# Five operand buffers in the down products of a transformer pair, and their neighbours in the order

## What is computed

```python
def conv_ffn(h, w_up, conv_w, conv_b, w_down):
    u = h @ w_up
    up = jnp.pad(u, ((0, 0), (CONV_WIDTH - 1, 0), (0, 0)))
    u = sum(up[:, i:i + T] * conv_w[i] for i in range(CONV_WIDTH)) + conv_b
    gate, val = jnp.split(u, 2, axis=-1)
    return (jax.nn.gelu(gate, approximate=True) * val) @ w_down

f = conv_ffn(rms_norm(h, norm_ffn_pre[l]), ffn_w_up[l], ffn_conv_w[l], ffn_conv_b[l], ffn_w_down[l])
h = h + rms_norm(f, norm_ffn_post[l])
...
def second_block(x, w_in, pool_w, pool_scale, attn_sinks, w_out, norm_pre, norm_post):
    h = rmsnorm(x, norm_pre[layer])
    proj = h @ w_in[layer]
    pool_u, pool_gate, q, k, v, attn_gate = jnp.split(proj, splits, axis=-1)
    pool_out = pool_mixer(pool_u, pool_w[layer], pool_scale[layer]) * jax.nn.silu(pool_gate)
    ...
```

## Time and profile before

| | us |
|---|---|
| median of three runs (lowest, highest) | 2544.6 (2544.19, 2546.92) |
| the profiled execution, its own time | 2542.34 |
| span of the profiled execution | 2540.5 |
| PE busy in the span | 2394.3 |
| DVE, POOL, ACT busy | 1269.2, 750.4, 694.0 |

### The profile page before, as it was taken

One profiled execution on the slowest core, in us unless ns is written; L12 is line 12 of the kernel. 1 busy time (PEld: TensorE's weight loads), 2 busy tenths in 40 slices (PEclk: granted clock), 3 DMA queues, 4 the chain that ended last, 5 costly groups with the idle time before them and its releaser, 6 DMA issues.

```text
span 2540.5 us, 33655 instructions
## 1 busy us (share of the span) xinstructions
PE 2394.3 (94%) x12944; PEld 1927.0 (76%) x12944; DVE 1269.2 (50%) x1446; ACT 694.0 (27%) x1076; POOL 750.4 (30%) x397
## 2 busy tenths in 40 slices
PE   5999999999999999999999999999999988989895
PEld 3788878877887887877787788888777766767674
DVE  6643263426434534766567544554421567636723
ACT  3422232222223113333243211111123444024421
POOL 1311231122113212113465333333244434322132
PEclk9999999999999999999999999999999999999997
DMA  3211111111111116545443111111143332111011
GB/s 122 70 42 59 68 50 56 53 59 59 51 59 59 50 50 194 185 145 191 141 158 116 42 50 50 41 50 50 41 150 98 108 95 76 53 50 42 26 42 66
DMA packets 58654, 201.00 MB, mean 79 GB/s; under 512 B 5936, under 2 KB 10160, under 8 KB 57776
## 3 DMA queue, kind: packets, MB, share of 16 engines
q1 hardware_dynamic: 39408, 134.56, 17.0%
q10 hardware_dynamic: 19136, 64.80, 6.8%
HBM read 163.16 MB, written 36.18 MB: 78 GB/s over the span
## 4 chain that ended last, share of the span: by engine, by line
PE 77%; DVE 12%; ACT 4%; DVEq 3%; issue 2%; DMA 1%; POOL 0%; ACTq 0%; POOLq 0%; SPq 0%
PE psg L442 10%; PE psg L441 10%; PE psg L437 10%; PE psg L570 5%; PE psg L568 5%; PE psg L563 5%; PE psa L660 1%; PE psg L1099 1%; PE psg L1104 1%; PE psb L649 1%; PE psg L1106 1%; PE psa L500 1%; PE psb L656 1%; DVE rw_SC L1337 1%; PE psg L466 1%
## 5 line engine op out<-in xcount | busy, mean ns | idle before, releaser
L378 POOL CAST whi<-wraw 128x1024 fp32r<-128x1024 f32 (+1 forms) x168 | 180.3, 1073 | 1537.9 <-PE psg L563 558.6
L380 POOL TENSOR_TENSOR wlo<-wraw,whi 128x1024 fp32r<-128x1024 f32 (+1 forms) x168 | 444.7, 2647 | 26.3 <-issue 6.3
L442 PE MATMUL psg<-xhi,wlo 128*128 128x512 f32 x1120 | 447.4, 400 | 0.0
L437 PE MATMUL psg<-xhi,whi 128*128 128x512 f32 x1120 | 441.7, 394 | 4.9 <-DVE pu L1754 2.6
L441 PE MATMUL psg<-xlo,whi 128*128 128x512 f32 x1120 | 442.8, 395 | 0.0
L570 PE MATMUL psg<-xhi,wlo 128*128 128x512 f32 x640 | 260.7, 407 | 0.0
L568 PE MATMUL psg<-xlo,whi 128*128 128x512 f32 x640 | 260.6, 407 | 0.0
L563 PE MATMUL psg<-xhi,whi 128*128 128x512 f32 x640 | 258.6, 404 | 0.0
L437 PEld LDWEIGHTS psg<-xhi,whi 128*128 128x128 f32 x1120 | 210.7, 188 | 57.6 <-issue 6.7
L441 PEld LDWEIGHTS psg<-xlo,whi 128*128 128x128 f32 x1120 | 210.8, 188 | 54.7 <-issue 0.7
L442 PEld LDWEIGHTS psg<-xhi,wlo 128*128 128x128 f32 x1120 | 210.8, 188 | 48.5
(11 more groups left out here) (549 smaller groups left out, 4527.8 us busy)
## 6 DMA issues: line engine op xcount, KB each, us to landing
wraw<-w SPq DMA_DIRECT2D x216, 512.0 KB, 3.6
later_scratch<-stage ACTq DMA_DIRECT2D x40, 512.0 KB, 2.6
xres<-xt ACTq DMA_DIRECT2D x4, 1024.0 KB, 10.8
RV<-later_scratch SPq DMA_DIRECT2D x4, 1024.0 KB, 11.9
RG<-later_scratch SPq DMA_DIRECT2D x4, 1024.0 KB, 6.3
later_scratch<-rstage ACTq DMA_DIRECT2D x8, 512.0 KB, 2.6
mgr<-later_scratch ACTq DMA_DIRECT2D x8, 512.0 KB, 3.9
mgt<-later_scratch ACTq DMA_DIRECT2D x8, 512.0 KB, 4.8
```

Of the source, the lines that this page charges most:

```text
L378: pool.tensor_copy(whi[:, u, 0:width], wraw[:, u, 0:width])
L380: pool.tensor_tensor(wlo[:, u, 0:width], wraw[:, u, 0:width], whi[:, u, 0:width].bitcast(F32), ALU.subtract).then_inc(w_ready, 1)
L437: mm = pe.matmul(ps[:, cols], whi[:, slot, w_cols], rhs_hi(k, cols), start=(k == 0), stop=False)
L442: mm = pe.matmul(ps[:, cols], wlo[:, slot, w_cols], rhs_hi(k, cols), start=False, stop=(k == kts - 1))
```

## The change

1. **Five buffers.** The operand parts of the second pass and of the tail go through a ring of `RING` = 5: two in the old place (now interleaved as `fparts`), three in `fhi_more` and `flo_more`, which lie in the first halves of `ff` tiles 16 to 21, read for the last time in the first pass. ACT and DVE make the parts three steps ahead of PE, and in a step ACT now copies the weights first.
2. **Residual tiles a step later on ACT.** The squares go two a step in steps 2 to 5, the sums on PE come after step 6 and the spread after step 8. DVE's `early_residual` starts in step 9, ACT's `early_high` in step 10, each one tile a step. The sums of the new squares (`mix_square`) stand in steps 18 to 21 instead of in the tail. In the tail a square follows each third part, as before.
3. **First step on the other banks.** The first `down` block takes output tiles 4 to 7 first, whose banks are not those that DVE still reads, and waits for the two others before tiles 0 and 2 only. DVE and ACT take the last hidden tile apart: gate taps ahead of the value, Gelu before the second weights copy, value behind it.
4. **Residual load in eight parts** of 512 KB, one after each pair of blocks.
5. **Second block.** `sums_of` of the second half comes after seven of the first `mix_block`'s eight slices, not after four. `pu` for pooled group 2 is taken from PSUM before DVE waits for group 1's map, and group 1 keeps its pooled values in `pu2`.

```diff
@@ -243,7 +245,9 @@
-        fhi, flo = tiles("fhi", 26, [P, 2, HALF], F32R), tiles("flo", 27, [P, 2, HALF], F32R)
+        fparts = tiles("fparts", 26, [P, 2, 2, HALF], F32R)
+        fhi, flo = fparts[:, :, 0, :], fparts[:, :, 1, :]
+        fhi_more, flo_more = tiles("fhi_more", 16, [P, 3, 2, HALF], F32R), tiles("flo_more", 19, [P, 3, 2, HALF], F32R)
...
+        def part_slot(two, more, n):
+
+            r = (n - FT) % RING
+            return two[:, r, :] if r < 2 else more[:, r - 2, 0, :]
...
@@ -952,10 +961,13 @@
-                for j in range(KT):
+                js = (4, 5, 6, 7, 0, 1, 2, 3) if start else range(KT)
+                for j in js:
                     w_cols = slice(j * P, j * P + P)
+                    if start and j in (0, 2):
+                        pe.wait_ge(g_free[j // 2], T_P2 // 2 + 1)
...
-            pe.wait_ge(g_free[0], T_P2 // 2 + 1)
-            pe.wait_ge(g_free[1], T_P2 // 2 + 1)
...
@@ -1001,10 +1012,10 @@
-                if k == 10:
+                if k == 6:
...
-                if k == 11:
+                if k == 8:
...
@@ -1025,10 +1036,10 @@
-            mix_block(0, range(KT // 2))
+            mix_block(0, range(KT - 1))
             pe.wait_ge(sem("down_added"), 2 * KT + 2)
             sums_of(psa[:, 0, :], dacc[:, HALF:T], NB // 2)
-            mix_block(0, range(KT // 2, KT))
+            mix_block(0, range(KT - 1, KT))
...
@@ -1630,17 +1641,40 @@
+            tt(fg[:, 1, :], psg[0][:, :], frs[:, :], MUL).then_inc(g_free[0], 1)
+            hidden_low(0, 0, 0)
+            taps(0, fg)
+            v.wait_ge(g_full, T_UP + 2 * FT)
+            tt(fv[:, 1, :], psg[1][:, :], frs[:, :], MUL).then_inc(g_free[1], 1)
+            v.drain()
+            hidden_low(0, 0, 1)
+            taps(1, fv)
...
@@ -1689,26 +1723,30 @@
-            for k in range(FT):
-                low(FT + k)
-                if 2 <= k < 2 + KT:
-                    down_square(0, k - 2)
-                if k == 11:
+            for n in range(FT, FT + RING):
+                low(n)
+            for k in range(2, FT):
+                low(FT + k + RING - 2)
+                if k < 2 + KT // 2:
+                    down_square(0, 2 * k - 4)
+                    down_square(0, 2 * k - 3)
+                if k == 7:
...
-                j = k - 12
+                j = k - 9
...
+                if 18 <= k:
+                    for q in range(2 * k - 35, min(2 * k - 33, KT)):
+                        mix_square(0, q)
+            for step in range(RING - 2, FT):
+                low(2 * FT + step)
+                if step >= 6 and step % 3 == 0:
+                    down_square(1, step // 3 - 2)
...
@@ -2213,24 +2256,32 @@
-            s.dma_start(dh[:, :, :], h_d).then_inc(sem("res_in"), 16)
-            with s.Fori(2, FT // 2) as i:
+            for i in range(2, 2 + DH_PARTS):
                 for u in range(2):
                     hidden_high(0, i, u)
                     weights_high(0, i, u)
+                js = slice((i - 2) * KT // DH_PARTS, (i - 1) * KT // DH_PARTS)
+                s.dma_start(dh[:, js, :], h_d[:, js, :]).then_inc(sem("res_in"), 16)
...
+                s.wait_ge(sem("f_used"), n + 1 if n < FT + 2 else max(FT + 2, n + 3 - RING))
...
@@ -2279,27 +2330,29 @@
+            for n in range(FT + 2, FT + RING):
+                part_high(n)
             for k in range(2, FT):
-                part_high(FT + k)
                 weights_part(B_DOWN + FT + k, EARLY * P)
...
+                part_high(FT + k + RING - 2)
...
-                if 12 <= k < 12 + KT:
-                    early_high(k - 12)
-            for k in range(FT):
-                part_high(2 * FT + k)
...
+                if 10 <= k < 10 + KT:
+                    early_high(k - 10)
+            weights_part(B_TAIL, 256 * TAIL[0])
+            for step in range(RING - 2, FT):
+                if step - RING + 1 in TAIL_AT[:-1]:
+                    c = TAIL_AT.index(step - RING + 1) + 1
                     weights_part(B_TAIL + c, 256 * TAIL[c])
...
+                part_high(2 * FT + step)
```

More of the change, by code:

```diff
@@ L72 @@
 B_TAIL = B_DOWN + 2 * FT
+RING = 5
+DH_PARTS = 8
 B_P2, T_P2 = B_TAIL + len(TAIL), T_UP + 2 * FT
@@ L964, in down_part @@
             def down_part(done, js, slot, col, begins):
-                u, k = done % 2, done % FT
+                k = done % FT
+                f_h, f_l = part_slot(fhi, fhi_more, done), part_slot(flo, flo_more, done)
                 pe.wait_ge(sem("f_split"), done + 1)
@@ L1067, in mixed @@
                 for half in range(2):
-                    mm = pe.matmul(psa[:, half, :], pw[:, :], pu[:, half * HALF:(half + 1) * HALF],
+                    mm = pe.matmul(psa[:, half, :], pw[:, :], (pu2 if g == 1 else pu)[:, half * HALF:(half + 1) * HALF],
                                    start=True, stop=True)
@@ L2215, in _ @@
             weights_high(0, 0, 0)
+            s.wait_ge(sem("cv_taps"), 2 * FT - 1)
+            act(fg[:, 0, :], fg[:, 0, :], ACT.Gelu_apprx_tanh).then_inc(sem("gelu"), 1)
+            weights_high(0, 0, 1)
+            s.wait_ge(g_free[1], T_UP // 2 + 1 + FT)
+            act(fv[:, 0, :], fv[:, 1, :], IDN, scale=cp[:, 6:7], bias=cp[:, 7:8]).then_inc(sem("cv_a"), 1)
             hidden_high(0, 0, 1)
-            value(FT - 1)
-            weights_high(0, 0, 1)
             for u in range(2):
```

76 lines of the change are left out of this document (43 added, 33 removed).

## The result

| | before | after |
|---|---|---|
| median of four runs each, side by side (lowest, highest) | 2545.45 (2544.19, 2546.92) | 2505.8 (2502.3, 2507.68) |
| the profiled execution, its own time | 2542.34 | 2507.68 |
| span | 2540.5 | 2505.9 |
| mean granted clock of TensorE over the span, of full | 0.986 | 0.987 |

The ratio after to before is 0.9841 with a 95% interval of 0.9829 to 0.9852: faster by 39.7 us. The forecast was 2509.5 with 2504 to 2523, so side and range held and the forecast was 3.7 us too high.

The account below looks back on a forecast made before the run. PE, busy 94% of the span, was taken as the bound, gains coming only from its waits and lowered clock. Terms 4.1 + 2.0 - 0.2 + 8.4 + 15.5 + 0.9 + 4.4 = 35.1 us gave 2544.6 - 35.1 = 2509.5, range 2504 to 2523.

Parts of the forecast that it names:

- The load: Residual load in the first pass: eight parts remove PE's wait for late weights, gain 2.0 us (0 to 2.0).
- the pooled groups: Pooled group 1: DVE empties the bank before the map is done, 4.5 instead of 8.90 us, gain 4.4 (2.9 to 4.5).
- The tail: Tail, 132 matmuls: five buffers remove PE's waits for held low parts, gain 15.5 us (10 to 16.5).
- Residual steps: Second pass, steps 12 to 21: weights first and later tiles gain 8.4 us (4 to 8.9), leaving 0.5 to PE.
- Start: Start of the down products: first block starts behind the last up matmul, gain 4.1 us (3.3 to 4.7).
- Second half's norm: Second half's norm: later sums lose their wait, 8.5 instead of 9.4 us, gain 0.9 (-0.5 to 1.8).
- Start of the second pass: Second pass, start: three more data parts on ACT ahead of step 2's weights, cost 0.2 us (0 to 0.8).
- DVE as the bound: Rival, residual steps and tail: DVE's work exceeds PE's time, 2520.7 us; chance 0.22.
- The clock staying down: Rival: PE's clock stays low though its waits are gone, 2515 us; chance 0.12.
- The parts of the load meeting the weights: Rival, residual load: each of eight parts stalls PE 2.0 us, 2525.5 us or less; chance 0.05.
- POOL not getting its turn: Rival: POOL's splits wait for DVE's whole row of 2.6 us, slower at 2570 us; chance 0.03.
- The ring bound by its splits: Rival, tail: splits, not data parts, bind it, so 10 of 15.5 us stay away, 2520 us; chance 0.03.

Follow-up runs that it names:

- one_load: Changed kernel with the residual loaded in one 4 MB transfer instead of eight parts; median 2505.94 us, third block to second pass 115.12 us against 113.04.
- old_pool: Changed kernel with pooled group 2's input taken from PSUM after group 1's map, as before; 2508.33 us, single execution.
- ring3: Changed kernel with three operand buffers instead of five; 2519.8 us, single execution, tail 41.56 us.
- ring2: Changed kernel with two operand buffers instead of five; 2533.43 us against 2544.3 before, tail 58.84 us.
- ring2_part: Changed kernel with two operand buffers and ACT making the data part ahead of the weights copy; 2524.74 us, single execution, tail 47.85 us.
- old_banks: Changed kernel with the first down block's output tiles in order 0 to 7 again, new DVE and ACT order kept; 2507.59 us, single execution.

## Where the prediction was right, and where not

**Right in its main mechanism.** The measure of 0.2333 us per matmul held in every stage, and the sum by stages, 35.1 us, met 37.2 (39.1 against the other execution of before). The prediction's "some 36 us are there to be had" is not the sum of its own list: 4.7 + 8.9 + 16.8 + 2.5, the pooled group's 4.4 and the load's 2.0 are 39.3. The forecast doesn't use it. The load (1.92 for 2.0) and the pooled groups (4.40 for 4.4) came out as worked out; one_load and old_pool took away just these (2.08 and 4.27).

**The tail, the term most mis-sized: 15.5 forecast, 16.67 measured.** The step that failed is DVE's sum of 33.6 us in 30.8, and the stall of about 1 us at part 10 laid out from it. DVE was busy for 24.94 us in the tail. The sum put the holds by POOL's subtractions at about 15 us, the whole of each; but only what is left of one when DVE's next operation is due is lost. Over their work of 0.64 or 0.69 us, the DVE operations held in the tail took some 9.9 us longer. The first long split shows it (POOL and DVE of the changed kernel, to be read against the pair in the earlier trace rows):

```profile
2062.65 2.90 POOL L415 TENSOR_TENSOR wlo<-wraw,whi 128x1024 fp32r<-128x1024 f32 x1 [1.89 <-ACT whi L2290]
...
2063.22 2.89 DVE L1676 TENSOR_TENSOR flo_more<-ff,fhi_more 128x512 fp32r<-128x512 f32 x1
```

The hold is the same as before (2.89 us for 0.7 of work), but DVE was there only at 2063.22 and PE, three parts behind, never saw it. DVE's last low part of the tail was through at about 2083.6, four microseconds ahead of PE's end. The other 0.3 of the forecast stalls, at the first long chunk, did not come either. Two and three buffers show how near the rival was: with one part of head start, 7.8 us of waits for DVE came back (ring3).

**Residual steps: 0.5 left to PE, 0 measured, and one step of the reasoning did not hold.** DVE was expected to slip by 1.3 us, then to need 4.0 us a step or less and stay there. It did not settle: from the second tile to the eighth its steps took 4.29 to 4.37 us against PE's 4.20, so it fell behind by 0.74 us in six steps and was still falling when the tiles ended. The ring covered this, and so did one part of head start (ring3). With no head start this pace is PE's: 4.33 to 4.36 us a step in ring2 and ring2_part. A step of the changed kernel on DVE, ACT and POOL, with the row of the tile five steps later:

```profile
2010.35 0.74 DVE L1699 SCALAR_TENSOR_TENSOR dy<-dy,prm,psb 128x512 f32<-128x512 f32 x1
2011.16 0.69 DVE L1701 TENSOR_TENSOR h<-dh,dy 128x512 f32<-128x512 f32 x1
2011.77 0.75 DVE L1693 SCALAR_TENSOR_TENSOR xlo<-h,prm,xhi 128x512 fp32r<-128x512 f32 x1
2012.43 2.35 DVE L1676 TENSOR_TENSOR fparts<-ff,fparts 128x512 fp32r<-128x512 f32 x1
...
2032.75 0.69 DVE L1701 TENSOR_TENSOR h<-dh,dy 128x512 f32<-128x512 f32 x1
...
2010.92 0.85 ACT L2290 ACTIVATE whi<-wraw 128x768 fp32r<-128x768 f32 x1 [1.70 <-PE psg L985]
...
2012.19 0.71 ACT L2302 ACTIVATE xhi<-h,prm 128x512 fp32r<-128x512 f32 x1
...
2011.94 2.29 POOL L415 TENSOR_TENSOR wlo<-wraw,whi 128x768 fp32r<-128x768 f32 x1 [2.07 <-ACT whi L2290]
```

ACT copies the weights first and has no wait before the tile (2.60 us in the earlier trace rows). POOL's 2.29 instead of 1.84 is one DVE operation in flight. The low part that pays the hold (2.35) is one that PE needs three steps later.

**Start: right in time, wrong in two causes.** The forecast stall at the third block was 0.6, the measured one 0.25: counted from the last up matmul, POOL's third split was through after 11.1 us instead of the 11.4 laid out, and DVE's low part, as laid out, about 0.6 behind it. The prediction also says that before, PE waited "until both low parts are made". It waited for the first: of the two that DVE makes from 1838.23 on in 1.29 us the first is through at about 1838.9, and PE started at 1839.07. And it had the first block start "on the free banks right behind the last up matmul". It did start there, but old_banks shows that it does so on the other banks too. What PE had waited for before is what the earlier trace rows names, DVE's low part; the value's bank was free by then. What the moved wait for this bank is worth in the new order is the open point named above.

**Second half's norm: 0.9 forecast, 1.24 measured.** Both new waits came, and both were smaller. The terms 0.6 + 4.9 up to the sums came as 5.32, the 2.3 from the sums to the spread as 2.21, and the 0.7 behind it as 0.41.

**Start of the second pass.** Cost 0.2; the second and third distances from block to block grew from 4.31 and 4.20 to 4.45 and 4.31, so 0.25.

**What lies between 35.1 and 39.7.** The gains above exceed their terms by 2.1 us. The profiled executions differ by 34.7; that of before lay 3.1 us below its median and that of after 1.9 above, which makes the 39.7. The prediction could allow for the first alone (it took 2.3 of three runs). Two executions of before differ by 1.9 us in the same stages, so the change is worth 37 to 39 us by its stages. The difference of the medians repeated (2545.49 less 2505.64 is 39.85), so what is left of it, 0.6 to 2.5 us, need not be scatter: it may lie in the stages of executions of before that have no trace. The runs don't show which.

**The rivals.** DVE as the bound: false with five buffers, true with three in the tail. The clock staying down: false, 1.00 in all five windows. The parts of the load meeting the weights: false, no wait there. POOL not getting its turn: false; in the residual steps its subtraction took 1.84 to 2.29 us, and in the step above it stood 0.45 us behind the one DVE operation in flight. The Trainium skill, "SBUF — State Buffer", SBUF: two separate sides, by which whoever starts first holds the shared port pair for the whole instruction, agrees with these rows: 0.7 us of low part lasted 2.35 to 2.89. The ring bound by its splits: false, 30.90 us. The rule weighed against the eight parts (the Trainium skill, "DMA: Bandwidth & Descriptors", Bandwidth: batch to 1 MiB or more) gave no cost here: a part of 512 KB landed in 4.5 us beside weights in 3.6, none was awaited, and the one transfer of 4 MB, which follows the rule, cost PE 2.1 us in one_load.

## What to carry to other kernels

When a producer shares its way to memory with another engine, size the buffers between it and PE by the longest hold in units of PE's step, not by its busy share: here 1.4 us steps and holds of up to 3 us wanted more than one part of head start, and three were enough. Take depth and order apart in experiments: with two buffers, weights first on ACT cost 11 us in the tail, and with five the same order ran at PE's pace. Look also for the move that does the work without the headline one: ACT's tile a step later, with the moves beside it, brought most of the second pass's gain with two buffers and the old order. And judge small parts by the distance between matmul starts, which repeated to 0.02 us where nothing waits, not by whole times: the executions of one kernel ranged over 7 us.

## What the runs showed of the hardware that was not expected

A memset on DVE is not held by POOL. In the changed kernel, DVE and POOL at the first down blocks:

```profile
1845.28 3.19 POOL L415 TENSOR_TENSOR wlo<-wraw,whi 128x1024 fp32r<-128x1024 f32 x1 [3.50 <-ACT whi L2243]
...
1844.97 1.23 DVE L1667 TENSOR_TENSOR ff<-fg,fv 128x1024 f32<-128x1024 f32 x1
...
1846.36 0.91 DVE L1185 MEMSET dacc<- 128x1024 f32 x1 [0.16 <-issue]
...
1847.19 1.82 DVE L1628 TENSOR_TENSOR fparts<-ff,fparts 128x512 fp32r<-128x512 f32 x1
```

POOL waits out the product that was in flight (3.19 us instead of 2.4). The memset then runs through in 0.91 us inside of POOL's subtraction, which ends at 1848.47, while the low part behind it lasts until 1849.0 for 0.7 of work.

What a wait costs through the clock depends on where the slow stretch falls. The same start of the same kernel, with the same wait of 2.19 us, took 16.15 us in one execution (granted clock 0.89) and 17.66 in another (0.90). The stretch at distances of 0.43 us was about as long in both, 3.3 and 3.4 us. In the first it lay in a block that ended in a wait anyway; in the second it lay behind that wait and was paid in full. Part of the gain of a removed wait is therefore a matter of the execution. What decides where the stretch falls is not shown.

Stages in which nothing was changed still move between executions: the part ahead of the down products took 1835.8 to 1841.5 us, the part behind 285.7 to 290.2, with mean granted clocks of the span between 0.983 and 0.990. What sets this was not tested.
